# Beside-work of the feed-forward stages moved by a slot, and eight modulation entries moved from l1_in to l1_out

## The reference

```python
mod = (silu_c @ w_mod[l] + b_mod[l])[:, None, :]           # of the tokens; mod_c of the context
sh_m, sc_m, gt_m, sh_f, sc_f, gt_f = jnp.split(mod, 6, axis=-1)
h = modulate(x, g_pre_mix[l], sh_m, sc_m)                  # rmsnorm(x, g) * (1 + scale) + shift
y, yc = even_mixer(h, hc, ...)  # layer 0;  odd_mixer in layer 1
x = x + gt_m * rmsnorm(y, g_post_mix[l])
h = modulate(x, g_pre_ffn[l], sh_f, sc_f)
x = x + gt_f * rmsnorm(swiglu(h, w_ffn_in[l], w_ffn_out[l]), g_post_ffn[l])
# in layer 0 the same for ctx with mod_c; swiglu is (silu(h Wg) * (h Wu)) Wo with 2816 hidden columns
```

## Time and profile before

| | us |
|---|---|
| median of 3 runs | 2820.28 |
| lowest, highest | 2819.4, 2821.28 |
| the profiled execution, its own time | 2820.28 |
| its span, first to last instruction | 2818.5 |
| PE busy in the span | 2734.4 |
| DVE, ACT, POOL busy | 1601.1, 1078.6, 1234.2 |
| mean granted clock of TensorE | 0.988 of full |

### The profile page before, as it was taken

The page is one execution under the profiler, slowest core; times in us unless marked ns, Lnnn a source line. Parts: engine busy times, 40 slices in busy tenths (PEclk is TensorE's granted clock), DMA queues, the critical chain, the costliest instruction groups (busy, mean ns, idle before and its releaser), DMA issues.

```text
span 2818.5 us, 41314 instructions
## 1 busy us (share of the span) xinstructions
PE 2734.4 (97%) x15742; PEld 2357.8 (84%) x15742; DVE 1601.1 (57%) x2593; ACT 1078.6 (38%) x1817; POOL 1234.2 (44%) x643
## 2 busy tenths in 40 slices
PE   8989999999999999999999999999999999999998
PEld 6778788788999899988888888888877788888887
DVE  6788576677776678455555555555553522422223
ACT  3267342223445357432222432222454833422222
POOL 0333454445566443345544355443433344444442
PEclk8999999999999999999999999999999999999999
DMA  5323555443576322234444244443323233133321
GB/s 237 108 46 102 189 197 189 157 142 114 200 253 218 132 65 61 76 105 153 166 160 158 96 138 166 159 171 111 112 61 105 82 98 98 63 101 97 97 90 60
DMA packets 103865, 361.70 MB, mean 128 GB/s; under 512 B 12449, under 2 KB 14625, under 8 KB 102305
## 3 DMA queue, kind: packets, MB, share of 16 engines
q1 hardware_dynamic: 103714, 359.63, 38.6%
HBM read 338.61 MB, written 2.10 MB: 121 GB/s over the span
## 4 chain that ended last, share of the span: by engine, by line
PE 85%; DVE 8%; ACT 3%; issue 2%; DMA 1%; POOL 1%; SPq 0%; DVEq 0%; ACTq 0%; POOLq 0%
PE ps L346 71%; PE ps L2255 3%; PE ps L2243 2%; PE ps L2225 2%; PE ps L750 1%; PE ps L570 1%; DVE negm L2304 1%; PE ps L422 1%; DVE dump L405 1%; PE ps L2448 1%; PE ps L2228 1%; PE ps L2013 1%; POOL w_lo L323 1%; DVE ps L834 1%; ACT prob L2277 0%
## 5 line engine op out<-in xcount | busy, mean ns | idle before, releaser
L323 POOL TENSOR_TENSOR w_lo<-raw,w_hi 128x1024 fp32r<-128x1024 f32 x421 | 1074.0, 2559 | 1207.5 <-ACT w_hi L317 1176.1
L317 ACT ACTIVATE w_hi<-raw 128x1024 fp32r<-128x1024 f32 x441 | 460.4, 1056 | 1158.1 <-PE ps L346 1109.1
L346 PE MATMUL ps<-n_hi,w_hi 128*128 128x512 f32 (+1 forms) x1744 | 639.5, 367 | 10.4 <-DVE n_lo L857 9.5
L346 PE MATMUL ps<-n_lo,w_hi 128*128 128x512 f32 (+1 forms) x1744 | 627.8, 360 | 0.0
L346 PE MATMUL ps<-n_hi,w_lo 128*128 128x512 f32 (+1 forms) x1744 | 627.8, 360 | 0.0
L346 PEld LDWEIGHTS ps<-n_hi,w_hi 128*128 128x128 f32 x1744 | 329.3, 189 | 66.8 <-DVE n_lo L857 9.8
L346 PE MATMUL ps<-h_hi,w_hi 128*128 128x512 f32 (+1 forms) x1096 | 364.7, 348 | 10.5 <-DVE h_lo L619 4.4
L346 PEld LDWEIGHTS ps<-n_lo,w_hi 128*128 128x128 f32 x1744 | 329.6, 189 | 51.0 <-issue 1.9
L346 PEld LDWEIGHTS ps<-n_hi,w_lo 128*128 128x128 f32 x1744 | 329.2, 189 | 49.2
L346 PE MATMUL ps<-h_lo,w_hi 128*128 128x512 f32 (+1 forms) x1096 | 356.7, 340 | 0.0
L346 PE MATMUL ps<-h_hi,w_lo 128*128 128x512 f32 (+1 forms) x1096 | 356.2, 340 | 0.0
(11 more groups left out here) (326 smaller groups left out, 3821.5 us busy)
## 6 DMA issues: line engine op xcount, KB each, us to landing
raw<-w_stream SPq DMA_DIRECT2D x441, 512.0 KB, 3.7
modraw<-mod_stream SPq DMA_DIRECT2D x128, 512.0 KB, 3.9
mod_extra<-mod_stream SPq DMA_DIRECT2D x48, 512.0 KB, 4.7
mod_pair<-mod_first SPq DMA_DIRECT2D x7, 1024.0 KB, 12.5
l_qs<-l_q_hi SPq DMA_DIRECT2D x32, 128.0 KB, 2.3
l_qs<-l_q_lo SPq DMA_DIRECT2D x32, 128.0 KB, 2.3
l_qs<-l_q_hi SPq DMA_DIRECT2D x16, 192.0 KB, 2.9
l_qs<-l_q_lo SPq DMA_DIRECT2D x16, 192.0 KB, 3.5
```

The source lines that it names most:

```text
L317: nc.scalar.activation(w_hi[:, c % RING, :], raw[:, c % RING, :], ACT.Copy).then_inc(hi_ready, 1)
L323: nc.gpsimd.tensor_tensor(w_lo[:, c % RING, :], raw[:, c % RING, :], w_hi[:, c % RING, :].bitcast(F32), ALU.subtract).then_inc(lo_ready, 1)
L346: mm = nc.tensor.matmul(out, w[a], x[b][:, off:off + n], start=first and i == 0, stop=last and i == 2)
```

## The change

The slots of both norms beside an FFN are moved later, mostly by one: the sum of the post norm from the end of group 1 to the middle of group 2, that of the pre norm from the end of group 6 to the middle of group 7, and squares, adds, root, products, scaled, high and low with them. ACT's square of chunk 4 of the pre norm moves from (5,0) to (6,0), its first added square on DVE from (5,0) to (5,1). The entries are spread otherwise: in the token FFN from group 4 on one in each (g, 0) and two in each (g, 1), up to (9, 1); in the context FFN one in each slot up to (9, 1). The numbers of entries of each stage stay. The eight entries of `l1_in` are loaded and reduced in `l1_out`: two before each of the copies of blocks 0 to 3, with bias and vectors after them; SP loads the first two right after attention and then two behind each of the weight loads n = 0 to 2.

```diff
-X_PARTS = ffn_parts(FFN_ENTRIES, [2] + [3] * 7 + [2] + [1, 2, 2, 2, 1, 2, 2, 2, 1, 2, 1, 0])
-C_PARTS = ffn_parts(X_PARTS[-1].stop, [1] * 6 + [2, 1, 2] + [1] * 10 + [0, 0])
+X_PARTS = ffn_parts(FFN_ENTRIES, [2] + [3] * 7 + [2] + [1, 2] * 6)
+C_PARTS = ffn_parts(X_PARTS[-1].stop, [1] * 21)
...
     def beside_pe(pe, post, pre, g):
-        if g == 1:
+        if g == 2:
             norm_sum_added(pe, post)
-        elif g == 6:
+        elif g == 7:
             norm_sum_added(pe, pre)
...
         at_ = (g, part)
-        squares_(post, src, y_there, {(0, 1): range(4), (1, 0): range(4, 8)}.get(at_, ()))
-        squares_(pre, stream_x, x_done(pre), {(4, 1): range(4), (5, 0): (4,), (5, 1): (5, 6), (6, 0): (7,)}.get(at_, ()))
-        if at_ == (1, 1):
+        if at_ == (0, 1):
+            squares_(post, src, y_there, range(4))
+        elif at_ == (1, 1):
+            squares_(post, src, y_there, range(4, 8))
+        elif at_ == (2, 1):
             norm_root(act, post)
+        elif at_ == (4, 1):
+            squares_(pre, stream_x, x_done(pre), range(3))
+        elif at_ == (5, 1):
+            squares_(pre, stream_x, x_done(pre), range(3, 4))
+        elif at_ == (6, 0):
+            squares_(pre, stream_x, x_done(pre), range(4, 6))
         elif at_ == (6, 1):
+            squares_(pre, stream_x, x_done(pre), range(6, 8))
+        elif at_ == (7, 1):
             norm_root(act, pre)
-        for k in {(7, 1): (0, 1), (8, 0): (2, 3), (8, 1): (4,), (9, 0): (5, 6), (9, 1): (7,)}.get(at_, ()):
+        for k in {(8, 0): (0, 1), (8, 1): (2,), (9, 0): (3, 4), (9, 1): (5,), (10, 0): (6, 7)}.get(at_, ()):
             norm_high(act, pre, slot, k)
...
-        for k in {(0, 1): (1, 2, 3), (1, 0): (4, 5, 6, 7)}.get(at_, ()):
+        for k in {(0, 1): (1, 2, 3), (1, 1): (4, 5, 6, 7)}.get(at_, ()):
             norm_added(dve, post, k)
-        if at_ == (1, 1):
+        if at_ == (2, 0):
             norm_turn(dve, post)
-        elif at_ == (2, 0):
+        elif at_ == (2, 1):
             norm_inverse(dve, post)
-        for k in {(2, 1): (0,), (3, 0): (1,), (3, 1): (2, 3), (4, 0): (4,), (4, 1): (5, 6), (5, 0): (7,)}.get(at_, ()):
+        for k in {(3, 0): (0,), (3, 1): (1, 2), (4, 0): (3,), (4, 1): (4, 5), (5, 0): (6,), (5, 1): (7,)}.get(at_, ()):
             norm_product(dve, post, post_slot, k, acc)
-        for k in {(5, 0): (1, 2), (5, 1): (3, 4), (6, 0): (5, 6, 7)}.get(at_, ()):
+        for k in {(5, 1): (1, 2), (6, 0): (3,), (6, 1): (4, 5, 6, 7)}.get(at_, ()):
             norm_added(dve, pre, k)
-        if at_ == (6, 1):
+        if at_ == (7, 0):
             norm_turn(dve, pre)
-        elif at_ == (7, 0):
+        elif at_ == (7, 1):
             norm_inverse(dve, pre)
-        for k in {(8, 0): (0, 1), (8, 1): (2, 3), (9, 0): (4,), (9, 1): (5, 6), (10, 0): (7,)}.get(at_, ()):
+        for k in {(8, 0): (0,), (8, 1): (1, 2), (9, 0): (3,), (9, 1): (4, 5), (10, 0): (6, 7)}.get(at_, ()):
             norm_low(dve, pre, slot, k)
-        for k in {(7, 0): (0, 1), (7, 1): (2, 3), (8, 0): (4,), (8, 1): (5, 6), (9, 0): (7,)}.get(at_, ()):
+        for k in {(7, 1): (0, 1), (8, 0): (2,), (8, 1): (3, 4), (9, 0): (5,), (9, 1): (6, 7)}.get(at_, ()):
             norm_scaled(dve, pre, slot, k)
...
                 in_block(pe, f, c + 1, d, up_bank, 1)
+            if beside:
+                beside(pe, g)
...
-                beside(pe, g)
                 return
...
             mm.then_inc(w_used, 2)
-            if beside:
-                beside(pe, g)
...
-    def halves_out_dve(dve, name, h, post_slot, slot):
+    def halves_out_dve(dve, name, h, post_slot, slot, before_chunk=None, after_chunks=None):
...
         for n in range(4):
+            if before_chunk:
+                before_chunk(n)
             dve.wait_ge(w_used, c0 + n + 1)
...
+        if after_chunks:
+            after_chunks()
         copy(0, 2)
...
-            for i in {3: (0,), 4: (1, 2), 5: (3, 4), 6: (5, 6), 7: (7,)}.get(p, ()):
-                mod_entry(dve, L1_ENTRIES + i, mod_slot(L1_ENTRIES + i))
...
-        mod_bias(dve, TAIL, 80, MOD_TAIL, modv_b[0], MOD1)
-        vectors(dve, modv_b[0], 0, 3, 1, 3, 4, None)
...
-        lambda sp, head: sp.wait_ge(mod_ops, mod_ops_before(TAIL)), l0_att, extra=l1_extra,
+        lambda sp, head: h_done(sp, "c_l1_pre"), l0_att, extra=l1_extra,
...
         attention_stream(l1_att)
         load_block(sp, FIRST["l1_out"] + RING - 1)
-        stage("l1_out")
+        for p in range(L1_ENTRIES, L1_ENTRIES + MOD_RING):
+            load_mod(sp, p)
+        for n in range(KC):
+            load_block(sp, FIRST["l1_out"] + RING + n)
+            if n < 3:
+                for p in range(L1_ENTRIES + 2 * n + 2, L1_ENTRIES + 2 * n + 4):
+                    load_mod(sp, p)
...
+        def l1_out_mods(n):
+            for p in range(L1_ENTRIES + 2 * n, L1_ENTRIES + 2 * n + 2):
+                mod_entry(dve, p, dump[:])
+
+        def l1_out_vectors():
+            mod_bias(dve, TAIL, 80, MOD_TAIL, modv_b[0], MOD1)
+            vectors(dve, modv_b[0], 0, 3, 1, 3, 4, None)
+
-        halves_out_dve(dve, "l1_out", 0, 0, 1)
+        halves_out_dve(dve, "l1_out", 0, 0, 1, l1_out_mods, l1_out_vectors)
```

More of the change, by code:

```diff
@@ L2109, in l1_in_dve @@
                 norm_low(dve, "c_l1_pre", 0, 4 * p - 9)
-            for i in {3: (0,), 4: (1, 2), 5: (3, 4), 6: (5, 6), 7: (7,)}.get(p, ()):
-                mod_entry(dve, L1_ENTRIES + i, mod_slot(L1_ENTRIES + i))
-            if p == 6:
+            elif p == 6:
                 dve.wait_ge(late_landed, 16)
@@ L2844, in _ @@
             load_block(sp, FIRST["l1_in"] + RING + i)
-            if i == 4:
-                sp.wait_ge(x_dve, 8 * (before("c_ffn_post", "_post") + 1))
-                load_mod(sp, L1_ENTRIES)
-                load_mod(sp, L1_ENTRIES + 1)
-            elif i > 4:
-                load_mod(sp, L1_ENTRIES + i - 3)
         h_done(sp, "c_l1_pre")
@@ L2948, in beside_x @@
         def beside_x(dve, g, part):
-            if (g, part) == (1, 1):
+            if (g, part) == (2, 0):
                 mod_bias(dve, FFN_ENTRIES + 8, MOD_FIRST, 24, modv_a[1], MOD0)
```

## The result

The changed kernel took 2836.06 us, median of 4 runs (2835.62 to 2836.5), against 2819.84 for the kernel before (4 runs, 2817.84 to 2821.28): ratio 1.006, 95% interval 1.0049 to 1.0073. It is slower by 16.2 us. The forecast was +8.7 us, with a range that ended at 2836.0: the time lies just outside it, slower as forecast, by nearly twice as much.

What follows compares the result with a forecast made beforehand. PE, busy 97% of the span, bounds the kernel, so only its waits and low-clock stretches count. Gains of 2.2, 1.1, 0.5 against costs of 5.3, 1.0, 0.4, 4.0, 1.0, 0.8 give +8.7: 2829.0 us, range 2824 to 2836 (8 in 10: 2819 to 2836).

Steps and rivals of the forecast that it cites:

- step 7: l1_out: weight block 7's load queues behind entry loads, so PE waits for post squares; +4.0 us, 2.2 to 6.5.
- Step 1: Token FFN group 5: slot (5,0) loses an entry and squares, so PE's wait for y goes; gain 2.2 us.
- Step 2: Context FFN group 5 to 6: later ACT square of chunk 4 ends a PE wait for w_lo; gain 1.1 us.
- Step 3: l1_in: with eight entries removed, PE no longer waits for the lows (h_lo); gain 0.5 us.
- Step 4: Token FFN's last group: entries in (9,1) and late lows lengthen PE's wait for ffn_lo; +5.3 us, 0.6 to 8.0.
- Step 5: Context FFN's last group: added work nearly cancels with freed bias and vectors, w_lo wait grows; +1.0 us, -0.6 to +5.
- Step 6: Norm sums moved to a group's middle: +0.2 us at each of two sums, +0.4 in all, at most 1.0.
- The clock: Low-clock stretches after PE's two long waits, token FFN end and l1_out: +1.0 and +0.8 us, nothing to 2.4 each.
- The locks fall well: Rival: no DVE instruction held by a split, no clock lost; -0.6 us, 2819.7 us; chance 0.25.
- The context end comes free: Rival: late splits let DVE finish before PE needs ffn_lo at context FFN's end; -6.9 us, 2813.4 us; chance 0.05.
- Only l1_out bites: Rival: only the half-out stage, or only the token end, costs; +3.0 us, 2823.3 us; chance 0.2.

Runs made afterwards that it cites:

- Experiment 6: Kernel before with only one pair entry moved from token FFN slot (5,0) to (8,0) and ACT's square 4 from (5,0) to (5,1): 2816.8 us against 2821.7.
- Experiment 3: Changed kernel with no entries in token FFN slot (9,1), its two placed at (6,0) and (8,0): 2835.1 us, +15.1 on the kernel before.
- experiment 8: Changed kernel with POOL's first four splits of the context FFN's weights cut to 8 of 1024 columns: 2830.4 us, +8.7 on the kernel before.
- first profile: The profiled execution of the changed kernel, nothing altered: 2833.18 us, span 2831.4.
- second profile: Profile of the changed kernel run again unaltered: span 2835.9 us; that run's median 2838.1 us against 2821.7 for the kernel before.
- experiment 4: Changed kernel with SP issuing l1_out's weight loads ahead of entry loads, DVE's order unchanged: 2829.6 us, +9.6 on the kernel before.
- 9: Changed kernel with each of DVE's four l1_out copies ahead of its two entries, SP's order unchanged: 2835.3 us against 2819.7 for the kernel before.
- Experiment 10: Changed kernel with both l1_out orders turned, weight loads ahead of entry loads and copies ahead of entries: 2825.0 us against 2819.7 for the kernel before.
- kernel 1: Kernel before with only the half-out part: eight entries, bias and vectors from l1_in to l1_out, staging moved: 2831.5 us, +11.5 on the kernel before.
- 11: Experiment 7's kernel plus the half-out part with weight loads and copies ahead of entries, gate vectors in l1_out: 2809.8 us against 2818.9 for the kernel before.
- 2: Changed kernel with the half-out part taken back, leaving the shift of norm work and FFN entries: 2827.1 us, +7.1 on the kernel before.
- experiment 7: Experiment 6's kernel with bias and vector write of context FFN slot (10,0) moved to the end of l1_in: 2812.4 us against 2821.7 for the kernel before.
- 12: Experiment 7's kernel run again on another chip session: 2813.1 us, 0.9971 of the kernel before.

## Why the prediction was right and where it failed

The forecast of 2829.0 us had the places and the chains of the loss right. Their sizes were too small, most of all that of step 7.

**Step 1, right.** -2.2 forecast, -2.5 measured (the column less the 0.5 of the moved sum). Experiment 6 has it alone.

**Step 2, right.** -1.1 forecast; experiment 6 has it alone with -1.4.

**Step 3, right.** -0.5 forecast, -0.8 in every kernel with the move and 0.0 without.

**Step 4, right in its mechanism, and nearly in its size.** The like slot of group 8 was a good model: 16.0 and two lows of 0.45 give 16.9 us from the last y add to the product, and it took 16.95. The wait grew by 5.8 us (0.4 to 6.2), not 5.3. The 0.7 that I took off for splits that would fall later was wrong: the first two reductions met no split, as I said, but the last two did, so three holds were there as in the like slot. Experiment 3 shows that the four reductions are its cause, experiment 8 that it is POOL's splits that hold them. The Trainium skill (SBUF — State Buffer, Who interferes with whom) has it that a two-input DVE instruction and a GpSimd instruction that reads SBUF exclude each other, and that the order of issue decides who waits. Experiment 8 agrees, 3.2 us against 1.23 for the same reduction, and so does the second reduction of the changed kernel, 1.23 us though a split began inside it.

**Step 5, right within its bounds.** +1.0 forecast, +1.3 and +1.6 measured with the clock. The wait for w_lo grew by 0.8 and the one for ffn_lo by 1.1; the clock gave 0.6 back in the first profile and 0.3 in the second. DVE in the changed kernel's last group of the context FFN, which answers to the earlier trace rows:

```profile
914.09 5.33 DVE L619 SCALAR_TENSOR_TENSOR h_lo<-nsq,vec_b,h_hi 128x512 fp32r<-128x512 f32 x2
...
921.91 0.17 DVE L465 TENSOR_TENSOR loaded<-loaded 128x16 f32<-128x16 f32 x1
922.12 0.17 DVE L474 SCALAR_TENSOR_TENSOR vec_g<-loaded 128x8 f32<-128x8 f32 x1
922.20 3.50 DVE L619 SCALAR_TENSOR_TENSOR h_lo<-tn,vec_b,h_hi 128x512 fp32r<-128x512 f32 x2
```

The bias and the vector write met no split, as the step said, and the added work and the holds of the lows took back what that freed.

**Step 6, too small.** +0.4 forecast, 1.0 measured, the most that the step allowed. At the second sum of the context FFN it is 0.4, at the first 0.6, of which 0.3 is a wait for the added squares; in the token FFN nothing. In the table this is hidden, since the stretch to g6 nets it against step 2.

**Step 7, the step that failed, by its size.** Its place, its chain and its side were right, as experiments 4, 9 and 10 show together: with the weights ahead the stage costs 1.8 us, with the copies first 9.8, with both nothing. But 4.0 was too little for a wait that came out at 6.0 and 6.5, at the top of the bounds of 2.2 to 6.5. Two parts of the working made the difference. I let the turns from entry 1 to entry 5 take 2 x 5.2 = 10.4 us, with reductions at 1.3; from 1176.09 to 1187.83 they took 11.7, since the first entry of each pair met a split (1.88 and 2.29). And I let block 7's load land in 3.7 to 5.4 us; beside two entry loads ahead of it and the next weight blocks behind it, it took 6.3. That the shared transfers make it 6.3 is argued; no run had that load alone. The first part is 1.3 us, the second 1.8 over the middle of what I allowed, which together is about the 3.0 us between 6.0 and the middle of 2.2 to 3.9. I had both rows, the long entries and the shared transfers, and kept them for the end of the range.

**The clock, mis-sized.** I took 1.0 and 0.8 us. Taken as what the delay grew by there, less the wait, the token FFN's end lost 1.7 and 2.3 us in the two profiles and l1_out 2.6 and 1.8. In the table's l1_out column the first profile shows 1.1 less, for the reason given there. The argument that part of the low stretch passes while PE waits held only at the first place, and even there about twice my 1.0 was lost.

**The sum.** With the touched stretches the change costs 12.6 us in the first profile (12.9 less +3.5, +0.0 and -3.2) and 14.5 in the second (17.4 less +0.7, +1.8 and +0.4), against 8.7. Of the 4 to 6 us between, l1_out with its clock is 2.8 to 3.8, and the token FFN's end 1.1 to 1.8. Added to 2820.3 us this is 2833 to 2835 us, near the end of my range but inside it. The median is 16.2 above the kernel before, 2 to 4 more than the touched stretches give, and my sum and my range had no term for those. What I can see of the rest is the clock in the attention. There the kernel before has one low stretch behind a wait of 1.8 us, and the second profile of the changed kernel one of about twice the length. Windows of PE (length, busy and count, PEclk, DMA share, GB/s), first before, then the second profile of the change:

```profile
1015.00:1020.00 5.00, 5.00 (x45) 0.70 0.23 55
1020.00:1025.00 5.00, 5.00 (x58) 1.00 0.00 0
```

```profile
1020.00:1025.00 5.00, 3.72 (x26) 0.68 0.45 105
1025.00:1030.00 5.00, 5.00 (x43) 0.64 0.01 3
```

The 1.8 to 2.1 us that this costs are in the second profile and in kernels 1, 3, 4, 8 and 9, not in the first profile, nor in 10 and 11, and in none of the kernels without the half-out part (2, 6, 7, 12). That part also moves the staging of q ahead of the attention, so this may be a cost of the change that my sum lacks, or chance. For chance speak the two profiles of the changed kernel, which differ there, and kernel 1's 1.6 us behind an unchanged wait. The staging was not run by itself, and it stays open.

**The rivals.** *The locks fall well* (0.25) did not come: entries met splits at both places. *The context end comes free* (0.05) did not come by the change either, but its price was real: experiment 7 frees most of it, 4.8 of the 6.3 us. *Only l1_out bites* fell, for experiments 1 and 2 each show a loss clear of its interval.

## What to carry to other kernels

Work that is moved beside other work is not free where its loads share an in-order queue with the weights: look at what is queued behind each wait, and put the loads that the bounding engine needs first. Experiment 10 makes the move of the eight entries nearly free by order alone; what the token FFN's end costs stays. And an instruction price that comes in two sizes is not taken at its median: find the engine that holds it, and price the slot by the neighbours that it will have.

## What the runs showed of the hardware

- The hold works both ways. A reduction of 128x1024 takes 1.23 us alone and 3.2 when it starts inside a split; a split that starts inside a reduction takes 3.0 us instead of 2.4 (709.10 and 712.38 us of the changed kernel), while the reduction that was running ahead of it takes no longer for it.
- The loss to the clock does not follow the wait's length. Waits of PE of 1.3 (experiment 4), 1.5 (7) and 2.3 us (8) were not directly followed by a low stretch. One of 2.2 us was followed by none in the kernel before and by a loss of 1.6 in kernel 1, for the same wait of the same code. One of 3.2 us (3) was followed by a loss of 1.9, one of 3.9 by 2.4, those of 5.9 to 6.5 by 1.5 to 2.6, one of 7.3 (1) by 3.1 and one of 8.4 (9) by 2.5. The 1.8 us at the start of the attention are followed by a low stretch in the kernel before and in most others, but not in kernels 7, 11 and 12.
- The stretch of low clock in the first 60 us, in code that no kernel changed, costs up to 3.9 us more in one kernel's profile than in another's.
